# Waits between the loads of an S5 layer: SyncE holds each load until the load of the same kind, one tile back, has landed

## The chip, the cores and the metric

The kernel runs on one core of a Trainium2 chip. The metric is the device time of one execution, in microseconds. Three runs of the kernel before gave a median of 2043.31 us, from 2042.37 to 2043.71.

## The reference

The reference is a two-layer streaming encoder over 256 tokens of width 2048, in float32. Each layer is a pre-normalised mixer with a residual, then a pre-normalised gated convolution FFN with a residual; a last RMS norm ends it. Layer 0 mixes with an mLSTM and gated linear attention side by side. Layer 1 mixes with an S5 layer, and only that one matters here:

```python
def s5_mixer(u, lam_re, lam_im, log_dt, b_re, b_im, c_re, c_im, d, w_glu, b_glu):
    ...
    lam_bar = jnp.exp(lam * dt)
    b_bar = ((lam_bar - 1.0) / lam)[..., None] * b
    ...
    def step(state, u_chunk):
        bu = jnp.einsum("gnp,btgp->btgn", b_bar, u_chunk.astype(jnp.complex64))
        a = jnp.broadcast_to(lam_bar, bu.shape)
        _, xs = lax.associative_scan(binop, (a, bu), axis=1)
        xs = xs + pow_t[None] * state[:, None]
        y = jnp.real(jnp.einsum("gpn,btgn->btgp", c, xs))
        return xs[:, -1], y
    ...
    y = jnp.moveaxis(y, 0, 1).reshape(B, L, Dm) + d.astype(f32) * uf
    y = jax.nn.gelu(y)
    y = y * jax.nn.sigmoid(y @ w_glu.astype(f32) + b_glu.astype(f32))
```

128 groups of 16 channels each drive a complex state of 64 numbers that runs through all 256 tokens; the outputs go through a GELU and a gated linear unit (GLU) with a 2048 x 2048 weight.

## The kernel before

Almost all of the time is dense products whose weights stream from device memory in 512 KB blocks through a ring of four (raw, split by ScalarE and VectorE into a high and a low part, hi and lo). Between the down projection of layer 0's FFN and the GLU of layer 1 lies the S5 part, some 66 us long, and the change is there alone.

The S5 part works in 16 tiles (kt 0 to 15) of 128 channels. The tokens are cut into 64 chunks of four. While the down projection runs, the core forms four operators for each tile and stores them in device memory. Each comes back by one load of SyncE (SP):

- p_op, 256 KB, `load_p` (L565, issue at L570): chunk inputs to states.
- rot, 256 KB, `load_rot` (L572, issue at L576): cosines and sines that turn the complex states so that the recurrence becomes a real scan.
- t_op, 128 KB, `load_t` (L579, issue at L584): inputs to outputs within a chunk.
- c_op, 256 KB, `load_c` (L587, issue at L592): states to outputs.

The normalised input comes back too, in eight loads of 256 KB (uu, `load_u`, L560). p_op, t_op and c_op have four slots each (OP_SLOTS), rot has eight (ROT_SLOTS). A load into a used slot first waits until the slot's last reader is done: x_done for p_op, y_done for t_op and c_op, xo_new for rot.

For a tile TensorE (PE) multiplies p_op by the input (chunk_states, L2340). VectorE (DVE) turns the states by rot (rotate_in, L1929; turned, L1935) and scans them (L1945). GpSimd (POOL) turns the result back (L958, two multiplications, and L961, a subtraction). PE then adds the t_op product (L2357) and the c_op product (L2369) into the outputs, which is chunk_outputs. The order on PE is written out: the states of tile kt, then the outputs of tile kt-3; the last three outputs follow at the end, and right behind them the GLU (glu_part, from L2394). After every second tile ScalarE (ACT) applies the GELU (L1331). After tiles 3, 7 and 11 it issues four SBUF-to-SBUF moves of 128 KB each (uu<-yg, L267) on its own DMA queue, and four of 64 KB after tile 13. They bring the outputs back into the order of channels.

SP carries out its loads strictly in the order of the program. Ahead of the loop they are written one by one (L597 to L631). In the loop over kt from 4 to 15 (L632) come p_op for kt+3, rot for kt+4, t_op for kt and c_op for kt. After tiles 7, 9, 11 and 13 one 512 KB block of GLU weights follows (`fetch`, L499). A load that waits for its slot holds up all that is written behind it. Nothing else limits how many loads are under way at a time.

Of the kernel before, what the change touches and what calls it, by code (L numbers as in the profile page):

```python
# [39 lines left out]
OP_SLOTS, ROT_SLOTS = 4, 8  # L40
# [66 lines left out]
def hybrid_encoder(nc, t, out):  # L107
# [6 lines left out]
    with ctx:  # L114
        def sem(name):
            return ctx.enter_context(nc.semaphore(name))
# [215 lines left out]
        p_full, c_full, t_full = ([sem(f"{x}_full{s}") for s in range(OP_SLOTS)] for x in ("p", "c", "t"))  # L332
        rot_full = [sem(f"rot_full{s}") for s in range(ROT_SLOTS)]
# [25 lines left out]
        def dve_split(v, b0, n, i, js):  # L359

            for j in js:
                s, _, _ = place(b0, n, j)
                v.wait_ge(hi_done, b0 + j + 1 + n * i)
                V.tensor_tensor(lo[:, s, :], raw[:, s, :], hi[:, s, :].bitcast(f32),  # L364
                                SUB).then_inc(lo_done, 1)

        def pe_tile(p, b0, n, i, j0, q, q_i, blocks, x2, ready, step=None, late=0):

            bank = acc[q % 2]
            if q >= 2 or not isinstance(q_i, int):  # L370
                p.wait_ge(tile_read, q - 1 + q_i)
            k, total = 0, sum(blocks)
            for m, nk in enumerate(blocks):
                s, _, _ = place(b0, n, j0 + m)
                p.wait_ge(lo_done, b0 + j0 + m + 1 + n * i)
                ready(k + nk)
                for x in range(nk):
                    w = slice(x * P, x * P + P)
                    if step is not None:
                        step(k)  # L380
                    if k >= total - late:
                        last = TE.matmul(bank[:, :], hi[:, s, w], x2(k)[:, :, :], start=False, stop=k == total - 1)
                    elif k == 0:
                        TE.matmul(bank[:, :], hi[:, s, w], x2(k)[:, :, :], start=True, stop=False)  # L384
                        last = TE.matmul(bank[:, L:], lo[:, s, w], x2(k)[:, 0, :], start=False, stop=False)  # L385
                    else:
                        TE.matmul(bank[:, L:], lo[:, s, w], x2(k)[:, 0, :], start=False, stop=False)  # L387
                        last = TE.matmul(bank[:, :], hi[:, s, w], x2(k)[:, :, :], start=False,  # L388
                                         stop=k == total - 1)
                    k += 1  # L390
                if late and k == total:
                    last.then_inc(half_done, 1)
                    for x in range(nk - late, nk):
                        last = TE.matmul(pb[1][:, 0:L], lo[:, s, x * P:x * P + P], x2(k - nk + x)[:, 0, :],
                                         start=x == nk - late, stop=x == nk - 1)
                last.then_inc(block_used, 1)
# [90 lines left out]
        def _(sp):  # L487
# [7 lines left out]
            def fetch(b0, n, i, j, src, width):  # L495
                s, _, _ = place(b0, n, j)
                if b0 + j >= RING or not isinstance(i, int):
                    sp.wait_ge(lo_done, b0 + j - RING + 1 + n * i)
                sp.dma_start(raw[:, s, 0:width], src).then_inc(raw_full[s], 16)  # L499
# [60 lines left out]
            def load_u(x):  # L560
                sp.wait_ge(u_out, 16 * (x + 1))
                sp.dma_start(uu[:, x // 2, :, x % 2 * 2:x % 2 * 2 + 2, :].rearrange("p m k c -> p m (k c)"),
                             u_dram[x, :, :].rearrange("(m x) (j n) -> (x j) m n", m=4, j=T5)).then_inc(u_in[x], 16)

            def load_p(kt):  # L565
                s = kt % OP_SLOTS
                sp.wait_ge(s5_dma_p, 32 * (kt + 1))
                if kt >= OP_SLOTS:
                    sp.wait_ge(x_done, kt - OP_SLOTS + 1)
                sp.dma_start(p_op[:, s, :, :].rearrange("p x n -> p (x n)"), s5_p[kt, :, :]).then_inc(p_full[s], 16)  # L570

            def load_rot(kt):  # L572
                s = kt % ROT_SLOTS
                if kt >= ROT_SLOTS:
                    sp.wait_ge(xo_new, kt - ROT_SLOTS + 1)
                sp.dma_start(rot[:, s, :, :, :].rearrange("p a m c -> p a (m c)"),  # L576
                             s5_rot[kt, :, :, :]).then_inc(rot_full[s], 16)

            def load_t(kt):  # L579
                s = kt % OP_SLOTS  # L580
                sp.wait_ge(s5_dma_t[kt % 2], 16 * (kt // 2 + 1))
                if kt >= OP_SLOTS:
                    sp.wait_ge(y_done, kt - OP_SLOTS + 1)
                sp.dma_start(t_op[:, s, :, :], s5_t[kt, :, :].rearrange("(m x) (j n) -> (x j) m n", m=4, j=T5)  # L584
                             ).then_inc(t_full[s], 16)

            def load_c(kt):  # L587
                s = kt % OP_SLOTS
                sp.wait_ge(s5_dma_c[kt % 2], 16 * (kt // 2 + 1))
                if kt >= OP_SLOTS:  # L590
                    sp.wait_ge(y_done, kt - OP_SLOTS + 1)
                sp.dma_start(c_op[:, s, :, :].rearrange("p x n -> p (x n)"), s5_c[kt, :, :]).then_inc(c_full[s], 16)  # L592

            def freed(groups):
                sp.wait_ge(block_used, B_GLU - len(DOWN_BLOCKS) + groups)

            freed(1)  # L597
            for x in range(2):
                load_u(x)
# [15 lines left out]
            freed(5)  # L615
            load_c(0)
            load_c(1)
            load_rot(2)
            load_rot(3)
            load_t(2)  # L620
            load_c(2)
            load_p(4)
            load_t(3)
            load_c(3)
            load_rot(4)
            load_p(5)
            load_u(6)
            load_u(7)
            load_p(6)
            for kt in range(5, ROT_SLOTS):  # L630
                load_rot(kt)  # L631
            for kt in range(OP_SLOTS, KT):  # L632
                if kt + 3 < KT:
                    load_p(kt + 3)
                if kt + ROT_SLOTS - OP_SLOTS < KT:
                    load_rot(kt + ROT_SLOTS - OP_SLOTS)
                load_t(kt)
                load_c(kt)
                if kt in (7, 9):
                    j = (kt - 3) // 2  # L640
                    fetch(B_GLU, 4, 0, j, w[j, :, :], BW)
                if kt in (11, 13):
                    j = (kt - 11) // 2
                    fetch(B_GLU, 4, 1, j, w[4 + j, :, :], BW)
# [1380 lines left out]
        def _(p):  # L2025
# [46 lines left out]
            def value_blocks(g, js):  # L2072

                banks = pb[4:6] if g % 2 == 0 else acc
                if js[0] == 0:
                    if g == 1:
                        p.wait_ge(tile_read, 17)
                    if g >= 2:
                        p.wait_ge(v_staged, g - 1)
                        p.wait_ge(v_copied, g - 1)  # L2080
                for j in js:
                    b = B_IN + 34 + V_BLOCKS * g + j
                    s, _, _ = place(b, 4, 0)
                    p.wait_ge(lo_done, b + 1)
                    for x in range(2):
                        k, w = 2 * j + x, slice(x * 4 * P, (x + 1) * 4 * P)
                        for half in range(2):
                            r = slice(half * P, (half + 1) * P)
                            TE.matmul(banks[half][:, :], xh[:, k, r], hi[:, s, w], start=k == 0, stop=False)  # L2089
                            TE.matmul(banks[half][:, :], xh[:, k, r], lo[:, s, w], start=False, stop=False)  # L2090
                            last = TE.matmul(banks[half][:, :], xl[:, k, r], hi[:, s, w], start=False,  # L2091
                                             stop=k == KT - 1)
                    last.then_inc(block_used, 1)
# [411 lines left out]
```

## Time and profile before

| | us |
|---|---|
| median of three runs | 2043.31 |
| lowest and highest | 2042.37, 2043.71 |
| the profiled execution's own time | 2044.81 |
| its span, first to last instruction | 2043.1 |
| PE busy in the span | 2005.1 (98%) |
| DVE busy | 1582.4 (77%) |
| ACT busy | 1127.3 (55%) |
| POOL busy | 571.7 (28%) |

All times of instructions are counted from the start of the span. Busy time is that of an engine's own instructions; waiting, branching and issuing DMAs don't count. The DMA queues are q1 for what SP issues, q10 for what ACT issues and q8 and q14 for instructions. Over the whole span PE is nearly always busy, so anything that the change does has to be read from the S5 part, between 1157 and 1224 us.

### The profile page before, as it was taken

The page shows a single profiled execution, that of the slowest core. Times are in us where ns is not written, and L with a number is a line of the kernel's source. Part 1 is how long each engine was busy: PE and PEld are TensorE (multiplying, and loading weights), DVE is VectorE, ACT ScalarE, POOL GpSimd, SP SyncE. Part 2 cuts the span into 40 slices and gives each one's busy share as a digit, 9 for nine tenths or more (in the row PEclk, how much of TensorE's full clock was granted, in tenths as well). Part 3 has the DMA queues.
Part 4 walks back from the last instruction along what each step waited for, and adds up shares of the span by engine and source line. Part 5 has one row for each costly group of instructions (what it writes and reads, how often), then busy time and mean ns, then how long its engine had stood idle before and what let it go on. Part 6 is the DMA issues. An engine that isn't in the chain of part 4 may idle for free.

```text
span 2043.1 us, 40986 instructions
## 1 busy us (share of the span) xinstructions
PE 2005.1 (98%) x13240; PEld 1751.3 (86%) x13240; DVE 1582.4 (77%) x2216; ACT 1127.3 (55%) x1655; POOL 571.7 (28%) x725
## 2 busy tenths in 40 slices
PE   7999999999999999999999989999999999999998
PEld 7877888888888888888888888888888888888886
DVE  7976678987888888878888887788888888865554
ACT  6544455466666566655555535666566565644443
POOL 8999014930000000037666772100000000001110
PEclk9999999999999999999999999999999999999999
DMA  6554435556666555557777985555555555566664
GB/s 238 164 186 165 166 124 175 187 194 207 215 209 202 192 186 188 192 165 237 237 234 235 309 238 180 194 195 191 189 186 192 187 187 192 182 185 190 187 192 134
DMA packets 147453, 398.82 MB, mean 195 GB/s; under 512 B 23344, under 2 KB 48688, under 8 KB 147392
## 3 DMA queue, kind: packets, MB, share of 16 engines
q1 hardware_dynamic: 126752, 379.30, 57.8%
q10 hardware_dynamic: 20640, 18.75, 2.8%
q8 instruction: 33, 0.54, 0.1%
q14 instruction: 28, 0.23, 0.0%
HBM read 377.02 MB, written 18.87 MB: 194 GB/s over the span
## 4 chain that ended last, share of the span: by engine, by line
PE 86%; POOL 8%; DVE 3%; issue 1%; ACT 1%; DMA 1%; SPq 0%; DVEq 0%; ACTq 0%; POOLq 0%
PE bank L388 50%; PE bank L387 25%; PE bank L384 3%; PE bank L385 1%; DVE lo L364 1%; PE bank L2089 1%; PE bank L2091 1%; PE bank L2090 1%; POOL nt L733 1%; DMA p_op<-s_p 1%; POOL nt L734 1%; POOL nt L732 1%; POOL nt L735 1%; PE bank L2369 0%; PE bank L2309 0%
## 5 line engine op out<-in xcount | busy, mean ns | idle before, releaser
L364 DVE TENSOR_TENSOR lo<-raw,hi 128x1024 fp32r<-128x1024 f32 x698 | 891.4, 1283 | 186.1 <-ACT hi L357 173.2
L357 ACT ACTIVATE hi<-raw 128x1024 fp32r<-128x1024 f32 x698 | 733.8, 1057 | 392.3 <-PE bank L388 332.2
L388 PE MATMUL bank<-aa,hi 128*128 128x512 f32 x2544 | 890.1, 392 | 0.0
L388 PE MATMUL bank<-xx,hi 128*128 128x512 f32 x2236 | 783.9, 392 | 0.0
L387 PE MATMUL bank<-aa,lo 128*128 128x256 f32 x2544 | 711.7, 280 | 0.0
L387 PE MATMUL bank<-xx,lo 128*128 128x256 f32 x2236 | 626.5, 280 | 0.9 <-DVE lo L364 0.9
L388 PEld LDWEIGHTS bank<-aa,hi 128*128 128x128 f32 x2544 | 477.5, 188 | 100.4
L388 PEld LDWEIGHTS bank<-xx,hi 128*128 128x128 f32 x2236 | 419.6, 188 | 87.3
L387 PEld LDWEIGHTS bank<-aa,lo 128*128 128x128 f32 x2544 | 478.8, 188 | 6.3 <-DVE lo L364 0.3
L387 PEld LDWEIGHTS bank<-xx,lo 128*128 128x128 f32 x2236 | 421.1, 188 | 8.4 <-DVE lo L364 2.2
L402 ACT ACTIVATE lowt<-bank 128x256 f32<-128x256 f32 x212 | 81.2, 383 | 210.5 <-PE bank L388 202.0
L407 DVE TENSOR_TENSOR sumt<-bank,lowt 128x256 f32<-128x256 f32 x212 | 89.7, 423 | 126.8 <-ACT lowt L402 126.7
L1791 DVE SCALAR_TENSOR_TENSOR cgv<-sumt,par,cgv 128x255 f32<-128x255 f32 x344 | 166.2, 483 | 27.4 <-DVE cgv L1791 12.5
L413 POOL TENSOR_TENSOR ssq<-h 128x256 f32<-128x256 f32 x2 | 2.3, 1157 | 512.8 <-DVE h L1758 496.4
L882 POOL MEMSET k_win<- 128x520 f32 x1 | 0.5, 532 | 461.1 <-PE bank L388 461.1
L1154 ACT ACTIVATE cgv<-sumt,par 128x256 f32<-128x256 f32 x172 | 103.6, 602 | 40.5 <-DVE sumt L1785 29.1
L416 POOL TENSOR_TENSOR sqt<-h 128x256 f32<-128x256 f32 x28 | 30.7, 1095 | 231.4 <-DVE h L1758 174.8
L1785 DVE TENSOR_TENSOR sumt<-sumt,bank 128x256 f32<-128x256 f32 x172 | 72.4, 421 | 5.8
L384 PE MATMUL bank<-xx,hi 128*128 128x512 f32 x132 | 54.3, 411 | 0.7 <-DVE lo L364 0.6
L384 PE MATMUL bank<-aa,hi 128*128 128x512 f32 x130 | 52.7, 406 | 0.7 <-issue 0.7
L2089 PE MATMUL bank<-hi,xx 128*128 128x512 f32 x128 | 51.7, 404 | 1.1 <-DVE lo L364 0.9
L908 POOL TENSOR_TENSOR sumt<-bbar,pow_in 128x256 f32<-128x256 f32 x64 | 51.9, 831 | 2.5
(384 smaller groups left out, 1902.5 us busy)
## 6 DMA issues: line engine op xcount, KB each, us to landing
raw<-in_up SPq DMA_DIRECT2D x344, 512.0 KB, 3.2
raw<-in_down SPq DMA_DIRECT2D x160, 448.0 KB, 3.6
raw<-in_w_in SPq DMA_DIRECT2D x98, 512.0 KB, 3.9
raw<-in_w_out SPq DMA_DIRECT2D x32, 512.0 KB, 3.4
raw<-in_down SPq DMA_DIRECT2D x32, 512.0 KB, 4.1
raw<-in_glu SPq DMA_DIRECT2D x32, 512.0 KB, 3.8
s_c<-cp ACTq DMA_DIRECT2D x16, 256.0 KB, 3.5
s_p<-ut ACTq DMA_DIRECT2D x32, 128.0 KB, 5.4
```

The lines of the kernel that those rows point to most:

```text
L357: A.activation(hi[:, s, :], raw[:, s, :], ACT.Copy).then_inc(hi_done, 1)
L364: V.tensor_tensor(lo[:, s, :], raw[:, s, :], hi[:, s, :].bitcast(f32), SUB).then_inc(lo_done, 1)
L384: TE.matmul(bank[:, :], hi[:, s, w], x2(k)[:, :, :], start=True, stop=False)
L387: TE.matmul(bank[:, L:], lo[:, s, w], x2(k)[:, 0, :], start=False, stop=False)
L388: last = TE.matmul(bank[:, :], hi[:, s, w], x2(k)[:, :, :], start=False, stop=k == total - 1)
L402: A.activation(lowt[:, q % 2, :], acc[q % 2][:, L:], ACT.Copy, **kw).then_inc(low_done, 1)
L407: return V.tensor_tensor(sumt[:, q % 2, :], acc[q % 2][:, 0:L], lowt[:, q % 2, :], ADD)
L908: ins = G.tensor_tensor(pq_pt[:, d], bbar[:, s, :, d, :].unsqueeze(3).broadcast_to([P, 4, S5_P, T5]), pow_in[:, pairs, :, (part + d) % 2]. ...
L1154: A.activation(o[:, :], sumt[:, (q_up + m) % 2, :], ACT.Identity, scale=par[:, bass.ds(base + 2, 1)], bias=par[:, bass.ds(base + 3, 1)]).t ...
L1785: V.tensor_tensor(x, x, pb[5][:, L:], MUL).then_inc(scaled_new, 1)
L1791: ins = V.scalar_tensor_tensor(o[:, d:L], x[:, 0:L - d], par[:, bass.ds(base + 2 - d, 1)], o[:, d:L], MUL, ADD)
L2089: TE.matmul(banks[half][:, :], xh[:, k, r], hi[:, s, w], start=k == 0, stop=False)
```

## The change

A helper `landed(full, slots, kt)` makes SP wait until the load of tile kt into one kind of operator has fully landed. It is put ahead of most of the S5 loads, with the load of the same kind one tile back as a rule. In the part written out some waits name another kind's load. In the loop p_op, rot, t_op and c_op each get one ahead of every load. Order, sizes and slots of the loads stay as they are, and so does everything on the other engines.

```diff
+            def landed(full, slots, kt):
+                sp.wait_ge(full[kt % slots], 16 * (kt // slots) + 16)
+
...
             load_c(0)
             load_c(1)
+            landed(p_full, OP_SLOTS, 3)
             load_rot(2)
             load_rot(3)
+            landed(rot_full, ROT_SLOTS, 1)
             load_t(2)
             load_c(2)
+            landed(c_full, OP_SLOTS, 0)
             load_p(4)
             load_t(3)
+            landed(c_full, OP_SLOTS, 1)
             load_c(3)
             load_rot(4)
+            landed(rot_full, ROT_SLOTS, 3)
             load_p(5)
             load_u(6)
             load_u(7)
+            landed(c_full, OP_SLOTS, 3)
             load_p(6)
             for kt in range(5, ROT_SLOTS):
+                landed(rot_full, ROT_SLOTS, kt - 1)
                 load_rot(kt)
             for kt in range(OP_SLOTS, KT):
                 if kt + 3 < KT:
+                    landed(p_full, OP_SLOTS, kt + 2)
                     load_p(kt + 3)
                 if kt + ROT_SLOTS - OP_SLOTS < KT:
+                    landed(rot_full, ROT_SLOTS, kt + ROT_SLOTS - OP_SLOTS - 1)
                     load_rot(kt + ROT_SLOTS - OP_SLOTS)
+                landed(t_full, OP_SLOTS, kt - 1)
                 load_t(kt)
+                landed(c_full, OP_SLOTS, kt - 1)
                 load_c(kt)
```

## Rows read from the trace of the kernel before

**Rows 1.** The chain of waits, 1157 to 1224 us: start us, us, what.
```profile
1193.79 0.24 SPq L576
...
1199.43 11.31 DMA p_op<-s_p
1210.75 0.14 issue
1210.88 1.16 PE bank L2340 x32
```

**Rows 2.** Timeline of POOL, from 1203 us: start us, us, engine, line, operation, operands, count [idle].
```profile
1203.55 2.49 POOL L958 TENSOR_TENSOR tab<-qq,rot 128x504 f32<-128x504 f32 x2
...
1206.80 2.50 POOL L958 TENSOR_TENSOR ut<-qq,rot 128x504 f32<-128x504 f32 x2
...
1210.60 2.51 POOL L958 TENSOR_TENSOR tab<-qq,rot 128x504 f32<-128x504 f32 x2 [0.50 <-PE bank L2369]
...
1214.61 2.50 POOL L958 TENSOR_TENSOR ut<-qq,rot 128x504 f32<-128x504 f32 x2 [0.70 <-DVE qq L1945]
```

**Rows 3.** Timeline of SP, the loads issued from 1160 to 1171 us.
```profile
1160.49 0.85 SPq L592 DMA_DIRECT2D c_op<-s_c  x1
1161.39 1.21 SPq L576 DMA_DIRECT2D rot<-s_rot  x1
...
1164.20 2.16 SPq L570 DMA_DIRECT2D p_op<-s_p  x1
1166.42 1.37 SPq L576 DMA_DIRECT2D rot<-s_rot  x3
1168.22 0.33 SPq L570 DMA_DIRECT2D p_op<-s_p  x1
1168.60 0.42 SPq L576 DMA_DIRECT2D rot<-s_rot  x1
...
1170.46 0.45 SPq L592 DMA_DIRECT2D c_op<-s_c  x1
```

**Rows 4.** DMA issues, 1161.3 to 1164.1 us: count, KB each, median us to landing.
```profile
uu<-u_dram SPq DMA_DIRECT2D x2, 256.0 KB, 7.1
c_op<-s_c SPq DMA_DIRECT2D x1, 256.0 KB, 7.3
rot<-s_rot SPq DMA_DIRECT2D x1, 256.0 KB, 7.1
```

**Rows 5.** DMA issues, 1178.6 to 1181.45 us.
```profile
c_op<-s_c SPq DMA_DIRECT2D x1, 256.0 KB, 3.6
p_op<-s_p SPq DMA_DIRECT2D x1, 256.0 KB, 2.9
rot<-s_rot SPq DMA_DIRECT2D x1, 256.0 KB, 3.1
t_op<-s_t SPq DMA_DIRECT2D x1, 128.0 KB, 2.8
```

**Rows 6.** DMA traffic, 1195.3 to 1200 us: packets, MB, mean rate.
```profile
DMA packets 1404, 1.69 MB, mean 359 GB/s; under 512 B 795, under 2 KB 795, under 8 KB 1404
```

**Rows 7.** DMA traffic, 1202 to 1206 us; queue: packets, MB, share of 16 engines.
```profile
DMA packets 1073, 0.81 MB, mean 202 GB/s; under 512 B 547, under 2 KB 924, under 8 KB 1073
...
q1 hardware_dynamic: 641, 0.42, 58.6%
q10 hardware_dynamic: 432, 0.39, 54.7%
```

**Rows 8.** Timeline of PE, 1156 to 1224 us: three c_op products.
```profile
1177.47 1.13 PE L2369 MATMUL bank<-ut,c_op 64*64 64x64 f32 x22 [1.98 <-issue]
...
1183.86 1.62 PE L2369 MATMUL bank<-ut,c_op 64*64 64x64 f32 x48
...
1221.42 1.98 PE L2369 MATMUL bank<-tab,c_op 64*64 64x64 f32 x48
```

**Rows 9.** Stretches: us, busy us of PE, PEld, DVE, ACT, POOL, granted clock, DMA share.
```profile
1177.90:1181.20 3.30, 3.30 (x70) 3.30 (x66) 0.86 (x2) 0.09 (x1) 2.46 (x2) 0.50 0.39 111
1181.30:1218.80 37.50, 31.69 (x1004) 30.51 (x1002) 34.38 (x65) 12.72 (x30) 34.09 (x31) 1.00 1.04 279
1218.90:1222.20 3.30, 3.30 (x68) 3.30 (x66) 3.30 (x4) 1.92 (x3) 0.00 (x0) 0.50 0.21 55
```

**Rows 10.** What SP itself waited for, 1136 to 1232 us: us, times, longest.
```profile
SPq L267 <- ACT yg L1331: 12.6, 1, 12.6
```

## The prediction

> **What bounds the kernel now.** I read the page first: over the whole span PE is busy 98%, so a change in SP's loads can only count where PE is not the bound, and that is the S5 part. There I read the chain of waits, then the timelines of POOL, SP and PE, then the DMA issues with their times to landing. In the chain [rows 1] the reader is to see SP's issues one behind the other from 1193.8 us on and then 11.31 us of a p_op load in flight (tile 15's), until PE takes the states at 1210.88. Around it POOL sets the pace: its back-turn starts at 1203.55 and 1206.80, 3.25 us apart, without a pause [rows 2]. The next two are late by 0.50 and 0.70 us, 1.2 us in all, behind PE and DVE that waited for late loads. So the part is bound by POOL at 3.25 us a tile, with a small loss to loads near its end.
>
> The loads are late there because the DMA engines are full: 1.69 MB went at 359 GB/s between 1195.3 and 1200 us [rows 6]. By that rate 256 KB (0.262 MB) take 0.73 us, 128 KB 0.37 us, a 512 KB block 1.46 us. The uu<-yg moves of ACT cost more than their bytes: from 1202 to 1206 us only 0.81 MB passed in 4.0 us, 0.42 MB of it loads [rows 7]. The loads alone would have taken 0.42 MB / 359 GB/s = 1.17 us, so 0.39 MB of moves took 2.83 us: 138 GB/s, 0.95 us for one of 128 KB.
>
> With a dozen loads queued one needs 7 to 11 us to land [rows 1, 4]; with four in flight and nothing behind, 2.8 to 3.6 us [rows 5].
>
> **The change part by part.** Fifty waits come in: six in the part written out, three ahead of rot 5 to 7, and in the loop 9 for p_op, 8 for rot, 12 each for t_op and c_op. Nothing is removed. As instructions they cost SP little: between issues that wait for nothing its rows leave about 0.05 us (1168.22 + 0.33 to 1168.60, [rows 3]), at most 2.5 us for all, spread beside the transfers. What counts is when the loads go out. Behind every waiting instruction stand all later loads, the GLU blocks and SP's share of the last moves; for them wait PE (p_op, t_op, c_op), DVE and POOL (rot), and ACT.
>
> *Up to rot 4.* The order stays and the queue is long (7 us to landing, [rows 4]), so a load that goes out up to 2 us later still finds a backlog and lands as before. Cost 0, and the backlog is the cover; were it gone, each such wait would cost its own 1 to 2 us.
>
> *rot 5 to 7.* Here the cover ends. c_op 3 lands at 1160.49 + 7.3 = 1167.8, so p_op 6 goes out at 1167.9 instead of 1164.20. rot 4 lands at 1161.39 + 7.1 = 1168.5, and rot 5 goes out at 1168.6 instead of 1166.42 [rows 3, 4]. In front of it are still the two u loads (to 1170.9) and p_op 6, so rot 5 lands about 1172.3. Then rot 6 must wait for it and travels alone: 1172.3 + 0.1 + 3.1 [rows 5] = 1175.5. rot 7 waits for that, and lands at 1178.7. Behind rot 7 stand p_op 7 (out at 1176.0, before 1168.22), rot 8 (1178.8, before 1168.60) and c_op 4 (1179.7, before 1170.46). The engines that were full before have little to do from 1172 to 1180. No consumer notices yet: c_op 4 lands about 1182.8 and PE multiplied by it at 1183.86 [rows 8]. But a lead of nine us in SP's order is gone, and 1 us is left.
>
> *The loop.* From here each round of p_op, rot, t_op, c_op lasts one landing of its slowest kind plus SP's wake-up, as every kind has one load in flight. By [rows 5] that is 2.9 us at the least (t_op's 2.8 plus 0.1) and 3.7 at most (c_op's 3.6 plus 0.1). I take 3.2, from rot's 3.1, as c_op's 3.6 holds an unusually long issue. That is POOL's pace, 3.25. Eleven rounds after c_op 4, c_op 15 would go out at 1179.7 + 11 x 3.2 = 1214.9 and land at 1218.0, ahead of the 1221.42 at which PE multiplied by it [rows 8].
>
> The GLU blocks and moves come on top. They are 4 x 1.46 = 5.8 us and, for the three sets of four moves before the end, 12 x 0.95 = 11.4 us, 17.2 in all. A round with three loads of 0.73 and one of 0.37 holds 2.55 us of transfers, so it has room for 0.65 us more. Seven rounds have that, the eighth (no rot) has 1.4, and the last three (t_op and c_op alone, 1.1 us) have 2.1 each: 12.3 us of room. The excess is thus 5 us if all of the room is used, 17.2 if none is. The moves come in sets of 3.8 us that stretch the round they fall in and the next, so the first two sets use 1.3 us of room and add 2.5 each; the third falls among the last rounds and finds room. Three GLU blocks add 0.8 each, the fourth nothing. Sum 5.0 + 2.4 = 7.4 us: c_op 15 lands at 1225.4, 4.0 us after it was used before.
>
> Before, a deep queue hid all this: the same bytes went with the engines full, and t_op and c_op of tiles 13 to 15 lay in line behind one another.
>
> *After it.* When PE stands for some 2 us its granted clock goes to 0.50 (1.2 of 2.4 GHz): that came after the 1.98 us pause at 1177.47 [rows 8, 9], and once more at 1218.9, two of four such stretches of 3.4 us in this part. Waiting for loads will bring one into the first GLU products. Half of 3.4 us would be 1.7; the stretch at the end exists already, so I add 1.0, with 0 and 1.7 as ends. The GLU blocks and last moves come later too, but SP stood 12.6 us before those moves [rows 10], and that covers it.
>
> **Sum:** 4.0 + 1.0 = 5.0 us slower. The profiled execution took 2044.81 us, 1.7 over its span and 1.5 over the median of the runs; it would take 2049.8, and the median goes from 2043.31 to 2048.3.
>
> **The rivals.** *Hidden.* The rounds last 2.9 us, the lower row. Then c_op 15 goes out at 1179.7 + 31.9 = 1211.6, lands unburdened at 1214.5, with 7.4 us of excess at 1221.9: 0.5 us late, 2043.8. For it speaks that p_op and t_op did land within 2.9 us [rows 5]; against it, that rot needed 3.1 and c_op 3.6, and that the slowest sets the round. By the Trainium skill (DMA: Bandwidth & Descriptors, section "Anatomy of one DMA — SWDGE (gpsimd) path") a transfer costs a fixed 2.0 us plus its bytes at 436 GB/s, an estimate of 2.6 us for 256 KB. By that rule a round is 2.7 us and the change is hidden; the rows, at 2.9 to 3.6, disagree, though the rule's point that a chain of single transfers pays the fixed part each time is what the rows show too.
>
> *Nothing happens.* Where SP waits for a slot anyway, a landing that comes sooner costs nothing. If that held from rot 5 on, the time stays at 2043.3. Against it: rot 5 to 8 have no slot to wait for in time, and went out back to back [rows 3].
>
> *Faster.* The deep queue itself is the harm. With short landings tile 14's and 15's loads are there in time, which gives back the 1.2 us of POOL [rows 2]; and the 1.98 us pause of PE in the middle of one tile's 48 c_op products, where nothing in the program waits [rows 8], may be code that came late through full DMA engines, worth 2.0 and, with the slow clock behind it, 1.65 more. Together 4.85 us: 2038.5. It decides if no round exceeds POOL's 3.25 us. Against it: the last rounds alone are four landings in a row after c_op 12.
>
> *Choked.* Rounds have no use of their room: the moves slow every load beside them, and all 17.2 us count. c_op 15 lands at 1235.2, 13.8 us late, which gives 2057.1. For it speaks the 202 GB/s in [rows 7]; against it, that POOL's pace leaves the moves time.
>
> **How the numbers follow.** The chances: forecast 0.52, hidden 0.22, nothing happens 0.06, faster 0.10, choked 0.10. About 0.2% (4 us) is what a measurement of this kernel can tell from no change. Slower beyond it are the forecast but for 0.04 of it, and choked: 0.58. Within it are hidden, nothing, that 0.04 and 0.03 of the faster case: 0.35. Faster beyond it: 0.07. The range takes in the forecast, hidden and nearly all of choked, and most of the small gains: 2042 to 2056.5, leaving out less than 0.1 at either end. The forecast alone spans 2045 to 2053.
>
> **What would show it.** In the changed kernel's trace rot 6 and rot 7 each land about 3 us after their issue and go out about 3 us apart from 1172 us on; DMA traffic falls in 1173 to 1180. c_op loads in the loop go out 3 to 5 us apart, land in 3 to 5 us instead of 8 to 11, and PE waits for c_op or t_op from about tile 8 on and for each of tiles 13 to 15. POOL's pauses grow. The first GLU product starts near 1228 instead of 1223.3. The prediction is wrong if c_op 15 lands before PE needs it, if POOL keeps 3.25 us to the end, or if the pause at 1177.47 goes and takes its 2 us along.

## The result: 14.6 us slower, and the profile after

The changed kernel took 2057.92 us (median of 3 runs, 2056.14 to 2058.98), against 2043.31 before: a ratio of 1.0073, with a 95% interval of 1.0059 to 1.0086. The forecast was 2048.3 with a range up to 2056.5. It had the sign and the place right and not half of the size. The profiled execution took 2057.92 us, its span is 2056.2 us; the one of before lay 1.5 us over its median, so between the two traces the change costs 13.1 us.

The first GLU product starts at 1236.07 us instead of 1223.33, 12.7 us later, so all but 0.4 us was lost in the S5 part. The chain of waits there, of the changed kernel (start us, us, what), answers to [rows 1]; the rows left out are issues of SP and PE's products:

```profile
1160.72 6.86 DMA rot<-s_rot
...
1167.60 3.69 DMA rot<-s_rot
...
1171.30 3.18 DMA rot<-s_rot
...
1174.50 3.19 DMA rot<-s_rot
...
1178.14 2.87 DMA t_op<-s_t
...
1181.03 7.37 DMA t_op<-s_t
...
1189.79 2.95 DMA c_op<-s_c
...
1192.76 4.61 DMA c_op<-s_c
...
1197.38 3.78 DMA c_op<-s_c
...
1201.18 5.86 DMA c_op<-s_c
...
1207.06 5.52 DMA c_op<-s_c
...
1212.60 4.29 DMA c_op<-s_c
...
1216.90 3.26 DMA c_op<-s_c
...
1220.17 4.07 DMA c_op<-s_c
...
1224.26 6.75 DMA c_op<-s_c
...
1231.05 2.83 PE bank L2383 x48
```

The reader is to see that from 1160 to 1231 us the chain is loads in flight and hardly anything else: one load at a time of rot, then t_op, then c_op, each put out within 0.05 us of the landing of the one before, but for 0.4 us at 1177.7 and 1.4 at 1188.4, both SP's own issues. Nothing computed on the chip stands in it. Before, SP's issues followed one another there and one transfer of 11.31 us came at the end.

What SP and PE waited for in the changed kernel (us in total, times, longest), SP from 1136 and PE from 1157 to 1245 us:

```profile
SPq L576 <- DMA rot<-s_rot: 14.9, 11, 3.3
SPq L584 <- DMA t_op<-s_t: 11.1, 6, 4.7
SPq L592 <- DMA c_op<-s_c: 8.0, 10, 1.9
...
PE bank L2371 <- DMA t_op<-s_t: 7.1, 4, 3.5
...
PE bank L2383 <- DMA c_op<-s_c: 6.0, 6, 2.0
```

SP's wait ahead of its last moves, 12.6 us before [rows 10], is 5.4 us now: the cover that the prediction named was used, and held. POOL's pauses (timeline; pause and releaser in brackets), to be read against [rows 2]:

```profile
1186.87 2.51 POOL L972 TENSOR_TENSOR ut<-qq,rot 128x504 f32<-128x504 f32 x2 [3.51 <-PE bank L2383]
...
1191.09 2.53 POOL L972 TENSOR_TENSOR tab<-qq,rot 128x504 f32<-128x504 f32 x2 [0.91 <-PE bank L2383]
...
1210.23 2.53 POOL L972 TENSOR_TENSOR tab<-qq,rot 128x504 f32<-128x504 f32 x2 [3.72 <-PE bank L2383]
1214.83 2.52 POOL L972 TENSOR_TENSOR ut<-qq,rot 128x504 f32<-128x504 f32 x2 [1.27 <-DVE qq L1959]
```

Both long pauses name PE as the releaser, and PE itself was behind the loads. SP's issues (timeline; x3 is three loads, with the waits between them inside the 7.23 us) answer to [rows 3]:

```profile
1167.60 7.23 SPq L576 DMA_DIRECT2D rot<-s_rot  x3
1174.94 0.36 SPq L570 DMA_DIRECT2D p_op<-s_p  x1
1177.70 0.33 SPq L576 DMA_DIRECT2D rot<-s_rot  x1
1178.14 0.46 SPq L584 DMA_DIRECT2D t_op<-s_t  x1
1178.70 0.44 SPq L592 DMA_DIRECT2D c_op<-s_c  x1
```

The three rot loads that took SP 1.37 us now take 7.23, and c_op 4 goes out 8.2 us later than at 1170.46. The stretches of the changed kernel (stretch, its us, busy us of PE, PEld, DVE, ACT and POOL, granted clock, DMA share, GB/s):

```profile
1171.00:1174.00 3.00, 3.00 (x110) 3.00 (x108) 2.93 (x7) 1.74 (x6) 2.92 (x4) 1.00 0.44 137
1174.00:1178.00 4.00, 4.00 (x136) 3.91 (x131) 4.00 (x9) 0.90 (x3) 3.58 (x5) 1.00 0.42 133
...
1202.00:1212.00 10.00, 6.46 (x161) 6.06 (x158) 4.86 (x10) 4.09 (x10) 5.71 (x6) 0.83 1.03 255
...
1227.90:1234.50 6.60, 4.57 (x80) 4.38 (x82) 5.04 (x5) 3.47 (x4) 0.00 (x0) 0.50 0.51 124
```

The DMA engines idle for more than half of 1171 to 1178 us and are full again at 1202 to 1212, with the second set of moves, while PE stands 35% and POOL 43% of that time. In the last row the clock stays at 0.50 for 6.6 us, against 3.3 at the end before [rows 9]. DMA issues of the loop at 1190 to 1194 us, with no moves beside them (count, KB each, median us to landing), answer to [rows 4, 5]:

```profile
c_op<-s_c SPq DMA_DIRECT2D x2, 256.0 KB, 3.8
raw<-in_glu SPq DMA_DIRECT2D x1, 512.0 KB, 5.5
p_op<-s_p SPq DMA_DIRECT2D x1, 256.0 KB, 3.4
rot<-s_rot SPq DMA_DIRECT2D x1, 256.0 KB, 3.4
t_op<-s_t SPq DMA_DIRECT2D x1, 128.0 KB, 3.4
```

A t_op of half the bytes takes as long as a p_op. PE's row that answers to the pause in [rows 8], two waits behind it, and the longest one:

```profile
1173.55 1.63 PE L2383 MATMUL bank<-ut,c_op 64*64 64x64 f32 x48
...
1179.91 1.17 PE L2354 MATMUL bank<-u_st,p_op 64*64 64x64 f32 x32 [1.73 <-DMA p_op<-s_p]
...
1183.89 2.83 PE L2383 MATMUL bank<-ut,c_op 64*64 64x64 f32 x48 [1.96 <-DMA c_op<-s_c]
...
1229.42 1.12 PE L2371 MATMUL bank<-uu,t_op 64*64 64x64 f32 x16 [3.51 <-DMA t_op<-s_t]
```

The 48 products are in one piece: PE's pause of 1.98 us is gone, and the tile that POOL began at 1182.88 before is begun at 1180.04, 2.8 us sooner. All of it was lost at the very next tile: PE stood 1.73 us for p_op 7 and 1.96 us for c_op 4, the loads behind rot 5 to 7, and POOL began that tile at 1186.87, where it had begun it at 1186.18 before.

### The profile page after: what moved, and what is told of

Same layout as the page of the kernel before. It is cut to its first block, busy times and chain, and to the rows that moved or that the text cites. A ratio compares the mean times of both kernels' runs of the same rounds, so it can differ in the third digit from the quotient of the medians.

```text
span 2056.2 us, 40996 instructions
## 1 busy us (share of the span) xinstructions
PE 2007.9 (98%) x13240; PEld 1753.1 (85%) x13240; DVE 1582.6 (77%) x2216; ACT 1127.4 (55%) x1655; POOL 573.8 (28%) x725
## 4 chain that ended last, share of the span: by engine, by line
PE 85%; POOL 7%; DMA 4%; DVE 3%; ACT 1%; issue 1%; SPq 0%; DVEq 0%; ACTq 0%; POOLq 0%
PE bank L388 49%; PE bank L387 25%; PE bank L384 3%; DMA c_op<-s_c 2%; PE bank L385 1%; DVE lo L364 1%; PE bank L2103 1%; PE bank L2105 1%; DMA rot<-s_rot 1%; PE bank L2104 1%; POOL nt L747 1%; POOL nt L748 1%; POOL nt L746 1%; POOL nt L749 1%; DMA t_op<-s_t 0%
## 5 line engine op out<-in xcount | busy, mean ns | idle before, releaser
L413 POOL TENSOR_TENSOR ssq<-h 128x256 f32<-128x256 f32 x2 | 2.3, 1156 | 517.6 <-DVE h L1772 496.5
L1881 DVE TENSOR_TENSOR cgv<-bc_in,powers 128x256 f32<-128x256 f32 x64 | 51.6, 845 | 0.0
```

The costliest lines, as they stand in the source:

```text
L1881: last = V.tensor_tensor(pq_cp[:, d], x.unsqueeze(3).broadcast_to([P, 4, S5_P, T5]), powers[:, bass.ds(4 * kt, 4), 0:T5, y].unsqueeze(2).b ...
```

## The experiments

Each time is a median, each ratio stands against runs of the kernel before on the same chip: 2042.77 us for the first five kernels below except for the one with late GLU blocks, 2042.63 for the next four, and 2042.86 for that one and the last three. Diffs are against the changed kernel unless the kernel before is named.

**Waits ahead of the loop alone.**

```diff
-                    landed(p_full, OP_SLOTS, kt + 2)
-                    landed(rot_full, ROT_SLOTS, kt + ROT_SLOTS - OP_SLOTS - 1)
-                landed(t_full, OP_SLOTS, kt - 1)
-                landed(c_full, OP_SLOTS, kt - 1)
```

> The changed kernel with the nine waits ahead of the loop alone; the 41 waits in the loop are taken out. Theory (the loss is the chain of landings in the loop; the gap that the waits on rot 5 to 7 make is harmless): no loss is left, and as the DMA queue is short when PE asks for new code, the 1.98 us pause of PE in the c_op products of tile 2 stays away as in the changed kernel; 2039 to 2043 us, the first GLU product starts at 1220 to 1223.5. Rival (the lead lost at rot 5 to 7 is what costs): some 8 us are still lost, 2049 to 2053 us.

Measured 2047.05 us (11 runs), ratio 1.0022 [1.0012, 1.0031]: 4.3 us slower, which neither theory gave. With no wait in the loop the nine ahead of it still cost something. POOL stood 4.50 us up to 1210.68, behind PE's products of tile 10, whose t_op load was 10.8 us in flight and landed at 1206.6.

**Waits in the loop alone.**

```diff
-            landed(p_full, OP_SLOTS, 3)
-            landed(rot_full, ROT_SLOTS, 1)
...
-                landed(rot_full, ROT_SLOTS, kt - 1)
                 load_rot(kt)
```

> The changed kernel with the 41 waits in the loop alone; the nine ahead of it are taken out, so the loop starts with c_op 4 out at 1170.5 instead of 1178.7. Theory (chain of landings, 4.76 us a round as measured in the changed kernel): the slots for t_op and c_op hold the first rounds back, so most of the 8 us of lead is lost in waiting for y_done, and the rounds from c_op 6 on at 4.5 to 4.8 us each give a last landing at 1223 to 1229; 2047 to 2053 us. Rival (the lost lead is what costs): 2043 to 2045 us.

Measured 2053.39 us (4 runs), 1.0053 [1.0038, 1.0068]: 10.6 us slower, just above the range of the theory. The two parts, 4.3 and 10.6, add up to 14.9, the whole change to 14.6. So the loop is the larger loss, and it doesn't need the late start: c_op 4 went out at 1175.43 here, 3.3 us sooner than in the whole change (though not at the 1170.5 expected), and c_op 15 at 1224.37. The sum doesn't show that the nine waits cost the same thing in the whole change as alone: alone they cost it in one pause behind a load of 10.8 us, and the whole change has no load of that length in its chain.

**Late GLU blocks.**

```diff
-                if kt in (7, 9):
-                    ... fetch(B_GLU, 4, 0, j, w[j, :, :], BW)
-                if kt in (11, 13):
-                    ... fetch(B_GLU, 4, 1, j, w[4 + j, :, :], BW)
+            for j in range(2, 4):
+                fetch(B_GLU, 4, 0, j, w[j, :, :], BW)
+            for j in range(2):
+                fetch(B_GLU, 4, 1, j, w[4 + j, :, :], BW)
```

> The changed kernel, but the four GLU blocks that the loop fetches are fetched behind the loop. Theory (in a chain of one load at a time every foreign transfer is paid for in full): from the issue of c_op 4 to that of c_op 15, 52.3 us in the changed kernel, 4 to 6 us go, so 46 to 48.5 us. Rival (a round has room, as the prediction had it): only 2.4 us go, so about 50 us. The kernel's whole time says less, since the GLU blocks are then late: 2050 to 2056 us by the theory.

Measured 2053.87 us (2 runs), 1.0051 [1.0033, 1.0069]. For these rounds one line serves: the twelve c_op issues of the loop (count; shortest, median and longest ns; first and last start us). The changed kernel, then this one:

```profile
L592 SPq DMA_DIRECT2D c_op<-s_c x12: 328/328/445, 1178.7 to 1231.0; - x12
```

```profile
L592 SPq DMA_DIRECT2D c_op<-s_c x12: 327/328/582, 1179.5 to 1226.0; - x12
```

From first to last 52.3 us became 46.5. The 5.8 us that went are what four blocks cost at the full rate of [rows 6], 4 x 1.46 = 5.84: by these two traces none of it was in the rounds' room, of which the rival took 3.4 us. The first GLU product starts 4.1 us sooner (1231.97).

**Moves cut to a quarter.** Three quarters of the moved outputs are left out here and in the kernels below that say so.

```diff
-            eng.dma_start(ych[..., k0 // 4, :, k0 % 4:k0 % 4 + k1 - k0, :], ...
-                          yg[:, k0 // 4, m, k0 % 4:k0 % 4 + k1 - k0, :] ...
+            eng.dma_start(ych[..., k0 // 4, 0, k0 % 4:k0 % 4 + k1 - k0, :], ...
+                          yg[0:2 * S5_P, k0 // 4, m, k0 % 4:k0 % 4 + k1 - k0, :] ...
```

> The changed kernel with a quarter of each uu<-yg move's bytes (the rows of one token in four; three quarters of the outputs are not moved, so that part is left out). It takes away three quarters of 11.4 us of moves. Theory (a chain of landings pays for every foreign transfer in full, no room is used): c_op 15 lands 8.5 us earlier than in the changed kernel, at about 1225, and the time falls to about 2049 us. Rival (as the prediction had it, moves partly fill idle time of the rounds): 3.8 us earlier, 1230, 2054 us.

Measured 2051.46 us (4 runs), 1.0044 [1.0029, 1.0058]. The same line:

```profile
L592 SPq DMA_DIRECT2D c_op<-s_c x12: 327/328/533, 1179.9 to 1224.3; - x12
```

The eleven rounds take 44.4 us, 7.9 less. Three quarters of 11.4 us (twelve moves at the 0.95 us worked out from [rows 7]) are 8.6. The time says less: the loss fell from 14.6 to 8.7 us, by 5.9, and c_op 15 went out 6.7 us sooner, both about midway between the theory's 8.5 and the rival's 3.8. The rounds differ from that because c_op 4 went out 1.2 us later here, ahead of any move.

**A bare loop:** moves cut to a quarter and GLU blocks late, both diffs above together.

> As e4_small_moves, and the four GLU blocks are fetched behind the loop instead of within it, so that hardly anything foreign is under way beside the rounds. Theory (foreign transfers in full, bare round 3.0 to 3.2 us as in the prediction): c_op 15 lands at 1217 to 1220, and the rounds of c_op are 3.0 to 3.4 us. Rival 1 (the bare round itself is longer, because SP's order ties the four kinds together): rounds of 3.7 us or more, c_op 15 at 1223 or later. Rival 2 (the prediction's use of room): rounds of 3.2 but the loss seen in e4 already gone, with no further gain from the GLU blocks.

Measured 2046.04 us (8 runs), 1.0016 [1.0006, 1.0026].

```profile
L592 SPq DMA_DIRECT2D c_op<-s_c x12: 327/328/443, 1178.7 to 1219.0; - x12
```

The rounds take 40.3 us, 3.66 each. The three between c_op 6 and c_op 9, with no move beside them, took 2.86, 4.09 and 3.43, so 3.46 on average; this is above POOL's 3.25 even with nothing foreign in the queue. The 3.66 lie between the theory (3.0 to 3.4) and the first rival (3.7 or more).

**Waits two tiles back in the loop:** two loads of a kind may be in flight. The nine waits ahead of it stay.

```diff
-                    landed(p_full, OP_SLOTS, kt + 2)
+                    landed(p_full, OP_SLOTS, kt + 1)
...
-                landed(c_full, OP_SLOTS, kt - 1)
+                landed(c_full, OP_SLOTS, kt - 2)
```

> The changed kernel with every wait of the loop one tile further back (kt+1, kt+2, kt-2, kt-2 instead of kt+2, kt+3, kt-1, kt-1), so two loads of a kind may be under way; the nine waits ahead of the loop stay. Theory (the loop's loss is a chain of single landings): two chains side by side halve the pace, about 52 us / 2 for eleven rounds against POOL's 36, so the loop's loss of 10 us goes and only the gap at rot 5 to 7 is left, 2046 to 2049 us, as with the waits ahead alone (2047.05). Rival (a queue of less than ten loads leaves the DMA engines underfilled as such): some 4 us more are lost, 2050 us or later.

Measured 2047.41 us (9 runs), 1.002 [1.001, 1.003], like the kernel without loop waits (2047.05). The loop's 10 us hang on the single load in flight, not on the waits as such.

**Only the six waits in the part written out.** The three ahead of rot 5 to 7 and the loop's are taken away.

> The changed kernel with the six waits of the part written out alone: the three ahead of rot 5 to 7 and the 41 of the loop are taken out. Theory (of the 4.3 us that the nine waits cost, the three in a row ahead of rot 5 to 7 cost all, as they empty the DMA engines; the six before find a backlog): no change, 2041 to 2044 us. Rival (it is p_op 6, 3 us later behind the wait for c_op 3, and what follows it that is missed): 2046 to 2048 us.

Measured 2042.29 us (11 runs), 0.9997 [0.9988, 1.0006]: no change. Its stretches show why; the DMA share (the number before the last) stays near full:

```profile
1171.00:1174.00 3.00, 3.00 (x98) 2.86 (x96) 2.93 (x7) 0.99 (x4) 2.82 (x4) 1.00 1.01 305
1174.00:1178.00 4.00, 2.84 (x96) 2.70 (x94) 3.41 (x8) 1.73 (x6) 3.05 (x4) 1.00 0.93 308
```

**Only the three waits of rot 5 to 7,** put into the kernel before.

```diff
             for kt in range(5, ROT_SLOTS):
+                landed(rot_full, ROT_SLOTS, kt - 1)
                 load_rot(kt)
```

> The kernel before with only the three waits ahead of rot 5, 6 and 7. Theory (these three empty the DMA engines for some 8 us and that work is missing later, when ACT's moves fill the engines): 2046 to 2048 us, and the DMA engines' share falls to about a half between 1172 and 1178 us. Rival (the six others did it): 2042 to 2044 us.

Measured 2048.25 us (7 runs), 1.0026 [1.0014, 1.0037]: 5.6 us for three waits. Here the engines do run empty:

```profile
1171.00:1174.00 3.00, 2.78 (x85) 2.57 (x83) 2.96 (x6) 0.72 (x2) 2.58 (x3) 0.98 0.31 69
1174.00:1178.00 4.00, 3.11 (x107) 2.97 (x103) 3.94 (x9) 2.38 (x7) 3.29 (x4) 1.00 0.58 175
```

and the price is asked for 30 us later, in POOL's longest pause of this kernel:

```profile
1212.07 2.52 POOL L962 TENSOR_TENSOR ut<-qq,rot 128x504 f32<-128x504 f32 x2 [3.91 <-PE bank L2373]
```

PE was waiting there for t_op 10. Its load took 8.8 us to land before and 10.8 here, and landed at 1207.94 instead of 1202.95: 3.0 us of that are its later issue (1197.18 for 1194.13), 2.0 its longer flight (its row of DMA issues: KB, us to landing; before, then this kernel):

```profile
t_op<-s_t SPq DMA_DIRECT2D x1, 128.0 KB, 8.8
```

```profile
t_op<-s_t SPq DMA_DIRECT2D x1, 128.0 KB, 10.8
```

**The kernel before with its last two GLU blocks late,** those of tiles 11 and 13 fetched behind the loop.

> The kernel before with the third and fourth GLU block of the loop fetched behind the loop instead of after tiles 11 and 13. Theory (in the last part the DMA engines are the bound, and foreign transfers ahead of p_op 14 to c_op 15 are paid in full): p_op 15 lands 1.4 us earlier, POOL's 1.2 us of pauses there shrink to half or less, 2041.5 to 2042.7 us, which is hardly to be told from before (2042.8). Rival (the blocks then come too late for the GLU): 2044 us or more, with PE waiting for lo in the first two GLU tiles.

Measured 2044.81 us (11 runs), 1.0012 [1.0003, 1.0021]. p_op 15 landed at 1208.86 instead of 1210.75 and POOL's two pauses at the end [rows 2] are gone. The pause of PE came sooner, 2.04 us at 1172.98, and held POOL for 2.90 at 1176.18. The time lies in the rival's range, but the cause that the rival named doesn't show: from 1222 to 1300 us PE waits for nothing. The loss of 2 us is not in this profile: the first GLU product starts at 1222.45, 0.9 us sooner than in the profiled execution of before, which was itself 1.5 over its median. Where it lies was not found (PE did stand 1.31 us up to 1221.37, amid the last tile's products, as it had not before), and a difference of 2 us between two single profiles says nothing.

**The gap with and without the moves.** Both kernels are the one before with the moves cut to a quarter; the first has the three rot waits as well.

> The kernel before with only the three waits of the rotary loads 5 to 7, and with the moves into the attention tiles cut to a quarter of their bytes (three quarters of the moved outputs are left out). To be read against e11_before_small_moves. Theory (the gap in the loads costs only because the DMA engines are full later, with the moves): at most 1 us over e11, both at 2036 to 2041 us. Rival (the lead that is lost is a direct cost, whatever comes later): 4 to 5.6 us over e11, as in e8.

> The kernel before with the moves into the attention tiles cut to a quarter of their bytes (three quarters of the moved outputs are left out), as the partner of e10_gap_small_moves. Both theories: 2036 to 2041 us, that is 2 to 6 us less than before, since the last eight tiles wait for loads that queue behind the moves; if the moves are hidden, 2042 to 2043 us.

Measured 2041.29 us with the gap (10 runs), 0.9991 [0.9981, 1.0], and 2042.24 without (10 runs), 0.9995 [0.9986, 1.0005]. The gap costs nothing: the rival, 4 to 5.6 us, falls. The level that both theories gave, 2036 to 2041, was too low; 2042.24 is what was set for moves that are hidden, and without the gap they are, to within 0.6 us. In the kernel with the gap POOL pauses once after 1182 us, and then holds its pace to the end:

```profile
1185.09 3.42 POOL L962 TENSOR_TENSOR ut<-qq,rot 128x504 f32<-128x504 f32 x2 [0.69 <-DVE qq L1949]
```

**A better version, tried.** rot 5 to 7 and the loop wait two tiles back, the loop only up to tile 7, and the GLU blocks of tiles 11 and 13 come behind the loop.

```diff
-                landed(rot_full, ROT_SLOTS, kt - 1)
+                landed(rot_full, ROT_SLOTS, kt - 2)
...
-                landed(t_full, OP_SLOTS, kt - 1)
+                if kt < 8:
+                    landed(t_full, OP_SLOTS, kt - 2)
...
-                if kt in (11, 13):
-                    ...
```

> The changed kernel with the waits of the rotary loads 5 to 7 and of the loop's loads on the load two tiles back, the loop's waits only up to tile 7, and the GLU blocks of tiles 11 and 13 fetched behind the loop; the six other waits ahead of the loop stay. Theory (two loads of a kind in flight keep the engines full, a short queue at the start spares TensorE its pauses of 1 to 3 us for code, and the last loads don't queue behind GLU blocks): 2038 to 2042 us. Rival (any wait on this path leaves the engines idle that are wanted later, or the pauses come at another place): 2043 us or more.

Measured 2046.72 us (11 runs), 1.002 [1.0011, 1.0029]. The theory was wrong in its sum. POOL did run without a pause from 1177.22 to 1204, but then it stood behind t_op 10 again (timeline of POOL):

```profile
1208.44 2.52 POOL L975 TENSOR_TENSOR ut<-qq,rot 128x504 f32<-128x504 f32 x2 [3.93 <-PE bank L2386]
```

The t_op load went out at 1194.02 and was 10.72 us in flight, between moves. Sparing PE its pauses brought the consumers forward, not the transfers. And PE stood once more, for no load, straight ahead of the first GLU product at 1224.81:

```profile
1223.74 1.14 PE L2386 MATMUL bank<-tab,c_op 64*64 64x64 f32 x30 [1.80 <-issue]
```

Behind the loop the late GLU blocks may cost what they cost in the kernel before, some 2 us; that share wasn't measured apart.

## Why the prediction was wrong

The mechanism was the one predicted, a chain of single landings, and one term of its sum was far too small. The rival "choked" gave 2057.1, with c_op 15 landing at 1235.2; it landed at 1233.69. That is near by luck in part: its eleven rounds and its 17.2 us make 52.4 us, against 52.3 measured, but the rounds were 2.5 us longer than it had them and the excess 2.6 us smaller. Step by step:

- **Up to rot 4, cost 0:** right. The six waits alone give 0.9997.
- **rot 5 to 7, the times:** right within 1.1 us (rot 5, 6, 7 at 1167.60, 1171.30, 1174.50 and c_op 4 at 1178.70, for 1168.6, 1172.4, 1175.6 and 1179.7).
- **rot 5 to 7, the price:** wrong. "No consumer notices yet" holds against the times of before, but PE was ahead of them by then and stood for p_op 7 and c_op 4, so the gain from its pause was gone. And the prediction counted the lost lead only through the rounds of the loop. Without any wait in the loop it costs 5.6 us (4.3 with the six others), and only with the moves whole: with quarter moves it is -0.95. That the transfers which the empty engines didn't carry at 1171 to 1178 us meet the moves after 1196 is the reading that fits; t_op 10, later and longer in flight, is its one row.
- **Rounds of 3.2 us:** somewhat low. The bare loop gives 40.3 us; less the quarter of the moves that is in it (a third of the 7.9 us that three quarters made, 2.6) that is 37.7, or 3.43 a round: 2.5 us more than 35.2.
- **The room of the rounds: the step that failed.** "The first two sets use 1.3 us of room and add 2.5 each; the third falls among the last rounds and finds room", and GLU blocks of 0.8 each: 7.4 us in all, of 17.2 that move. From c_op 4 to c_op 15 it was 52.3 us, so 52.3 - 37.7 = 14.6 us of excess, 85% of the 17.2 (that it equals the whole slowdown is chance). The moves carry 10.5 of it by one pair (7.9 x 4/3), 8.3 by the other (46.5 to 40.3, 6.2 x 4/3); the GLU blocks 4.1 (44.4 to 40.3) or 5.8 (52.3 to 46.5). Each of these is the difference of two single traces, and the two pairs differ by some 2 us, so the shares are good to no more than that. The error in c_op 15's landing, 8.3 us (1233.69 for 1225.4), is 7.2 from this step (14.6 for 7.4) and 2.5 from the rounds, less 1.0 as c_op 4 went out sooner and 0.4 as the last load landed faster. The last three rounds, said to find room for the third set and the fourth GLU block, took 3.27, 4.09 and 6.76 us.
- **The slow clock, 1.0:** too much. c_op 15 landed 12.3 us after its use before (1233.69 for 1221.42) and the first GLU product came 12.7 us later, so 0.5 us is left for all that follows the landing. Tile 14's c_op product took 2.83 us at 0.50, but it had taken nearly as long before, in the stretch of [rows 9]:

```profile
1218.37 2.46 PE L2369 MATMUL bank<-ut,c_op 64*64 64x64 f32 x48 [2.14 <-POOL ut L961]
```

- **The pause of PE at 1177.47:** the prediction said it could go and take its 2 us along. It went, and POOL gained 2.8 us by 1180, but gave them back at the next tile, which waited for PE and PE for loads.

The prediction summed bytes: a round of 3.2 us with 2.55 us of transfers has 0.65 free. The runs show that this room was hardly used. Why is argued: the part of a landing that is no transfer can't be filled by foreign bytes for the chain's benefit, as each kind's next load goes out only when its last has landed, and a foreign transfer that has come into the engines by then stands ahead of it. In the changed kernel the rounds with moves in them are the long ones of the chain: 7.37 us from 1181.03 on, beside the first set (issued from 1178.84), 5.86 and 5.52 us at 1201 to 1212, where the second set was in flight, and 6.75 from 1224.26 on, with parts of the third, of the next and of a GLU block.

The Trainium skill (DMA: Bandwidth & Descriptors, section "Anatomy of one DMA — SWDGE (gpsimd) path") puts most of the fixed part of a DMA on the gpsimd path, which these loads don't take, into the confirmation that the last byte has landed. The rows fit a large fixed part here too: 128 KB of t_op and 256 KB of p_op both took 3.4 us in one stretch. They don't show where in the path it lies.

What stays open: why PE pauses for 1 to 3 us amid a group of products in which nothing in the program waits (1.98 us before, 2.04 with late GLU blocks, 2.92 up to 1183.25 with the six waits, 1.80 in the better version). A deep queue of loads can't be all of it: in the better version SP had put out its last load by 1212.07 and two GLU blocks right behind, some 10 us ahead of the pause. The traces do show what comes just before PE goes on. On q8, a queue for instructions, a packet of 16 KB is through at 1176.2, 1171.6, 1181.8 and 1222.5 us, and PE goes on at 1177.47, 1172.98, 1183.25 and 1223.74, 1.3 to 1.4 us later each time. That speaks for PE's code coming late, as the rival "faster" supposed; what held it up is not shown.

## What to carry to other kernels

A load that waits for its predecessor makes a chain of landings: price every other transfer that passes through the same engines in the meantime nearly in full (85% here), and leave two in flight per chain (two back cost nothing more here, one back 10 us). Where engines are full later, an idle stretch of theirs earlier is not free, even if no consumer waits during it: ask which bytes will now travel beside the burst. And test such a pair of causes as a two by two, since each of them alone cost nothing here.

## What the runs showed of the hardware

- **Two causes that cost only together.** Three waits that leave the engines idle for some us, and twelve moves from SBUF to SBUF later on:

| | moves whole | moves a quarter |
|---|---|---|
| no waits | 2042.63 to 2042.86 | 2042.24 |
| three rot waits | 2048.25 | 2041.29 |

- **ACT's moves did not share the engines with SP's loads from the start.** In the kernel before ACT issued four moves from 1196.20 us on, but in 1195.3 to 1200 us its queue q10 moved no packet; the only queue in the list is SP's (packets, MB, share of 16 engines):

```profile
q1 hardware_dynamic: 1404, 1.69, 107.8%
```

  They landed 6.9 to 8.9 us after issue, at 1203.05 to 1207.01. The Trainium skill (DMA: Bandwidth & Descriptors, section "Queues, rings and completion order") says that an engine goes round between the queues it has work for, packet by packet. With free engines a move of this kind, of 64 KB, landed 2.3 us after its issue (SP's first one in the kernel before). If the moves were in their queue as soon here, packets of q10 should by that rule have passed by 1198.5; the row shows none up to 1200. Whether the engines did not go round, or q10 had nothing for them yet, it doesn't show.
- **Slow clock at the end.** The 0.50 stretch of 3.3 us before became one of 6.6 us (1227.9 to 1234.5). PE had then stood since 1225.9 for a t_op; it came back at 1229.42 and stood another 0.51 us for a c_op.
